# Three weight buffers instead of two, six gathered tokens instead of eight, and later transfers in SyncE's queue

## The chip, the cores and the metric

The kernel runs on one core of one Trainium2 chip. The metric is the device time of one execution in microseconds, given as the median of several runs. The engines are TensorE (PE; its weight loads are PEld), VectorE (DVE), ScalarE (ACT), GpSimd (POOL) and SyncE (SP). Sixteen DMA engines move data between HBM and SBUF; two queues feed them here, SyncE's and GpSimd's.

## What is computed

Two transformer blocks in a row over 256 tokens of width 1024, batch 1, float32. The first has attention with 8 heads of 64, a spatial gating unit and a feed-forward layer. The second has two layers over the tokens (x) and a context of 256 tokens (ctx). Each layer is a mixer (latent attention, a Fourier branch, a convolution branch, merged by gates) and then an expert layer:

```python
    def chunk(hc):
        q = (hc @ w_query).reshape(PEER_CHUNK, PEER_HEADS, 2, D_KEY // 2)
        s = jnp.einsum('chpd,hpnd->chpn', q, sub_keys).astype(jnp.float32)
        s_top, i_top = lax.top_k(s, PEER_TOPK)
...
        best, pos = lax.top_k(cand, PEER_TOPK)
        eid = jnp.take_along_axis(cand_id, pos, axis=-1)
        gate = jax.nn.softmax(best, axis=-1).astype(hc.dtype)
        u = jnp.take(u_tab, eid, axis=0)
        act = jax.nn.gelu(jnp.einsum('chkd,cd->chk', u, hc)) * gate
        v = jnp.take(v_tab, eid, axis=0)
        return jnp.einsum('chk,chkd->cd', act, v)
```

Each token picks 8 x 16 = 128 rows of `u_tab` and 128 rows of `v_tab`, 4 KB each: 0.524 MB per table and token. 768 token steps (ctx layer 0, x layer 0, x layer 1) make 805 MB of gathered rows. Shifts, scales and gates of every norm come from a modulation: a vector times a 1024 x 6144 matrix (`adaln`, and the same in the first block).

## The kernel before, in words

**Weights.** `chunks` is the list of all weight tiles in the order in which TensorE uses them: large ones of 2 MB (1024 x 512) and small ones of 0.5 to 1 MB. SyncE loads tile i into `W[:, i % RING]`, RING = 2, and waits for `w_used` of tile i - RING, which TensorE signals behind a drain (L368) in `done_with_weights`. A merge goes through pairs: a large gate tile ("zg") against H, then a small branch tile ("wb"). There are four merges: "c0" (context, layer 0), "f" (first block), "x0", and "x1", whose stretch has no gathers. In SyncE's queue other transfers stand between the weight tiles: `xT`, the mask, `wsgT` and eight pieces of `b_sgu` (they wait for `idx_ready` 2, the end of the second route), and the sub-keys (they wait for `att_ready`).

**Modulation.** `MODS` lists 18 modulations of 4 MB each, in two halves ("chunks") of 2 MB. All run in the first mixer "c0" and its route, at the places of `MODS_AT`: 0 and 1 at "n1", 2 at "zf", 3 at "dc", 4 at "v", 5 at "heads", 6 at "roots", 7 at "normed", 8 to 12 in the merge, 13 to 17 in the steps "top 0" to "keys 0" of the first route. The halves lie in UV, the buffer of the gathered rows, which is not used before: 4 x 16 KB per partition. GpSimd loads them (L1940) and waits for `rows_copied`, which ScalarE signals when it has copied a modulation's rows to `yfill`. TensorE's `modulation` (matmuls at L508) waits for both halves, then turns the rows of the modulation before it (L492); VectorE's `add_rows` (L1030) adds them.

**Gathered rows.** Visit g handles tokens 2g and 2g + 1. GpSimd gathers U rows (L1961) into slot tok % SLOTS, at most three visits ahead, when `dots` says that token tok - SLOTS is done, and V rows (L1971) when `outputs` says that visit g - SLOTS/2 is done. TensorE spreads the token's h over the partitions (L404), VectorE takes the dot products (L968), ScalarE the gelu, VectorE multiplies by the gate, TensorE sums the V rows (L419) two visits later. Visits are laid into TensorE's program by an estimate, `beat`: one visit per PACE = 7.4 estimated us of products, and at the end of each segment the rest in one stretch (`stream`, `close_stream`). 256 visits belong to segment 0, 128 to segment 1. All of SBUF that matters here is W (RING x 16 KB per partition) and UV (2 x SLOTS x 4 KB).

Of the kernel before, what the change touches and what calls it, by code (L numbers as in the profile page):

```python
# [25 lines left out]
NEXP = NKEY * NKEY  # L26


SLOTS = 8
GROUP = 32  # L30
PAIRS = P // 2
FILL = 64
# [32 lines left out]
def two_blocks_kernel(nc, A, out):  # L65
# [7 lines left out]
    with ctx:  # L73
# [5 lines left out]
        def sem(name):  # L79

            if name not in sems:
                sems[name] = ctx.enter_context(nc.semaphore(name))
            return sems[name]
# [1 line left out]

        X = sb("X", [P, DT, TALL])
        H = sb("H", [P, DT, SEQ])
        RING = 2
        W = sb("W", [P, RING, 4096])
        KC = sb("KC", [QK, MH, SEQ])  # L90
        VC = sb("VC", [P, 2, 512])
        UV = sb("UV", [P, 2 * SLOTS, D])
        hs = sb("hs", [96, 2, 4, D], bf16)
        acts = sb("acts", [P, SLOTS, 2 * GROUP - 1])
        yfill = sb("yfill", [P, 512])
        dots = sb("dots", [P, SLOTS])
        gel = sb("gel", [P, SLOTS])
        idxT = sb("idxT", [P, 2, P], u32)
# [47 lines left out]

        Us, Vs = UV[:, 0:SLOTS, :], UV[:, SLOTS:, :]

        def mod_chunk(i):
            return UV[:, 4 * (i % 4):4 * (i % 4) + 4, :].rearrange("p a b -> p (a b)").rearrange("p (k n) -> p k n", n=512)  # L150


        q1 = view(0, 4, SEQ)
# [87 lines left out]
        MODS = [("l", 0, m) for m in range(6)] + [("ada", 0, m) for m in range(6)] + [("l", 1, m) for m in range(6)]  # L241
# [12 lines left out]
        def cols(ap, j):  # L254
            return ap[:, :, j * 512:(j + 1) * 512]
# [45 lines left out]
        def ring_slot(i):  # L301
            _, _, kt, n = chunks[i]
            return W[:, i % RING, 0:kt * n].rearrange("p (k n) -> p k n", n=n)

# [20 lines left out]
        def _(pe):  # L325
# [3 lines left out]
            pool = list(range(NBANK))  # L329
# [78 lines left out]
            def outputs(g):  # L408
# [5 lines left out]
                for tok in (2 * g, 2 * g + 1):  # L414
                    pe.wait_ge(sem(f"v_arrived{tok % SLOTS}"), 16 * (tok // SLOTS + 1))
                for tok in (2 * g, 2 * g + 1):
# [78 lines left out]
            def modulation(u, flush=False):  # L495

                o = bank(("mr", u))
                if u == 0:
                    pe.wait_ge(sem("cond_ready"), 1)
                w = [mod_chunk(2 * u + j) for j in range(2)]  # L500
                for j in range(2):
                    i = 2 * u + j
                    pe.wait_ge(sem(f"mod_arrived{i % 4}"), 16 * (i // 4 + 1))
                for kk in range(4):
                    for j in range(2):
                        for kh in range(2):
                            q = 32 * (2 * j + kh)
                            last = mm(o[q:q + 32, :], cond32[:, 4 * kh + kk, :], w[j][:, 4 * kh + kk, :], start=(kk == 0), stop=(kk == 3))  # L508
                full(last, ("mr", u))
                if pending:  # L510
                    turn_rows()
                pending.append(u)
                if flush:
                    turn_rows()
# [378 lines left out]
        @block.sync  # L893
        def _(sp):
            sp.dma_start(vec[:, :], A["vec"]).then_inc(sem("vec_loaded"), 16)
            sp.dma_start(ident[:, :], A["ident"]).then_inc(sem("ident_set"), 16)
            sp.dma_start(X[:, :, 0:SEQ], A["ctxT"]).then_inc(sem("ctx_loaded"), 16)

            def weight(i):
                if i >= RING:  # L900

                    sp.wait_ge(sem("w_used"), i - RING + 1)
                sp.dma_start(ring_slot(i), chunks[i][1]).then_inc(sem(f"w_arrived{i % RING}"), 16)

            sp.wait_ge(sem("mod_arrived3"), 16)
            for i in range(RING):
                weight(i)
            sp.dma_start(dftc[:, :, :], A["dftc"]).then_inc(sem("const_loaded"), 16)
            sp.dma_start(ropet[:, :, :], A["rope"][:, :, SEQ:]).then_inc(sem("const_loaded"), 16)
            sp.dma_start(rotm[:, :], A["rotm"]).then_inc(sem("const_loaded"), 16)  # L910
            sp.dma_start(gqk[:, :], A["gqk"]).then_inc(sem("const_loaded"), 16)
            sp.dma_start(iota16[:, :], A["iota16"]).then_inc(sem("const_loaded"), 16)
            attended = {"c0": 8, "x0": 24, "x1": 32}
            for i in range(RING, len(chunks)):
                weight(i)
                what = chunks[i][0]
                if what == ("inC", "c0") or what == ("inB", "c0"):
                    sp.dma_start(X[:, :, SEQ:], A["xT"]).then_inc(sem("x_loaded"), 16)
                if what == ("in1", 1):

                    sp.wait_ge(sem("idx_ready"), 2)
                    sp.dma_start(mask1, A["mask"]).then_inc(sem("mask_loaded"), 16)
                    sp.dma_start(wsg1, A["wsgT"]).then_inc(sem("wsg_loaded"), 16)
                    for p in range(4):
                        for a in range(2):
                            sp.dma_start(bsg1[64 * a:64 * a + 64, p, :], A["b_sgu"][0, 2 * p + a:2 * p + a + 1, :].to_broadcast([64, P])).then_inc(sem("bsg_loaded"), 16)
                if what[0] == "wb" and what[1] in attended and what[2:] == (0, 0):

                    sp.wait_ge(sem("att_ready"), attended[what[1]])
                    sp.dma_start(keys, A["keys"][LAYER[what[1]]]).then_inc(sem("keys_loaded"), 16)  # L930
            sp.wait_ge(sem("added"), 12)
            sp.dma_start(out, X[:, :, SEQ:]).then_inc(sem("stored"), 16)
            sp.wait_ge(sem("stored"), 16)
# [995 lines left out]
        @block.gpsimd  # L1929
        def _(pool):  # L1930
            def load_mods(u):

                which, l, m = MODS[u]
                src = rows(A["w_ada"][0] if which == "ada" else A["w_mod_2"][l])
                for j in range(2):
                    if u >= 2:

                        pool.wait_ge(sem("rows_copied"), u - 1)
                    i = 2 * u + j
                    pool.dma_start(mod_chunk(i), cols(src, 2 * m + j)).then_inc(sem(f"mod_arrived{i % 4}"), 16)  # L1940

            for u in range(2):
                load_mods(u)
            pool.wait_ge(sem("ones_set"), 1)
            pool.affine_select(out=tri[:, :], in_=ones[:, :], compare_op=ALU.is_ge, fill=0.0, base=0,
                               pattern=[[1, P]], channel_multiplier=-1).then_inc(sem("tri_set"), 1)
            for u in range(2, len(MODS)):
                load_mods(u)
            pool.wait_ge(sem("rows_copied"), len(MODS))

            def gather_u(g):

                if 2 * g % P == 0:
                    pool.wait_ge(sem("idx_ready"), 2 * g // P + 1)
                for tok in (2 * g, 2 * g + 1):
                    j = tok % SLOTS
                    if tok >= SLOTS:
                        pool.wait_ge(sem("dots"), tok - SLOTS + 1)
                    pool.sem_inc(sem("pool_paced"), 1)
                    off = bass.IndirectOffsetOnAxis(idxT[:, tok // P % 2, tok % P:tok % P + 1], 0)  # L1960
                    pool.indirect_dma_start(Us[:, j, :], None, A["u_tab"], off).then_inc(sem(f"u_arrived{j}"), 16)  # L1961

            def gather_v(g):

                if g >= SLOTS // 2:
                    pool.wait_ge(sem("outputs"), g - SLOTS // 2 + 1)
                pool.sem_inc(sem("pool_paced"), 1)
                for tok in (2 * g, 2 * g + 1):
                    j = tok % SLOTS
                    off = bass.IndirectOffsetOnAxis(idxT[:, tok // P % 2, tok % P:tok % P + 1], 0)  # L1970
                    pool.indirect_dma_start(Vs[:, j, :], None, A["v_tab"], off).then_inc(sem(f"v_arrived{j}"), 16)  # L1971

            asked = 0
            for g0, g1 in SEGMENTS:
                for g in range(g0, g1):
                    for ahead in range(asked, min(g + 3, g1)):
                        n = ahead // PAIRS
                        if ahead > g and ahead % PAIRS < 2 and ready_at[n] > PAIRS * n - 2:
                            break
                        gather_u(ahead)  # L1980
                        asked = ahead + 1
                    gather_v(g)
# [72 lines left out]
```

## Time and profile before

| | |
|---|---|
| median of 3 runs | 3815.41 us (3814.5 to 3819.07) |
| profiled execution | 3841.13 us, its span 3839.4 us |
| PE busy | 2670.4 us (70%) |
| PEld busy | 1375.4 us (36%) |
| DVE busy | 1781.0 us (46%) |
| POOL busy | 1478.2 us (39%) |
| ACT busy | 497.7 us (13%) |
| DMA | 1047.09 MB, mean 273 GB/s |
| granted TensorE clock, mean | 0.786 |

The profiled execution is one run with the hardware profiler on, and somewhat longer than the median. The first 480 us are "c0" and its first route, then the first block and the mixer "x0" with visits among the products, from about 1830 to 2620 mostly visits, from 2620 to 3070 the mixer "x1" without visits, and to the end visits alone. The mean GB/s hides these stretches.

### The profile page before, as it was taken

How to read it: one execution, taken by the hardware profiler on the slowest of the kernel's cores; microseconds unless marked ns; L12 is line 12 of the kernel's file. 1: busy time of each engine (PE TensorE's matmuls, PEld its weight loads, DVE VectorE, ACT ScalarE, POOL GpSimd, SP SyncE). 2: the span in 40 equal slices, each digit the busy share in tenths (PEclk: the TensorE clock that was granted, in tenths of full speed). 3: DMA queues.
4: the chain of work that ended last, by engine and by line, in shares of the span. 5: the costliest groups of instructions: out<-in, count | busy, mean ns of one | idle time of the engine just before them, and what ended most of it. 6: DMA issues, size and time to landing. Idle time of an engine off the chain costs nothing.

```text
span 3839.4 us, 35128 instructions
## 1 busy us (share of the span) xinstructions
PE 2670.4 (70%) x11672; PEld 1375.4 (36%) x11672; DVE 1781.0 (46%) x4443; ACT 497.7 (13%) x1114; POOL 1478.2 (39%) x1577
## 2 busy tenths in 40 slices
PE   7798676889998888784565555557788455555555
PEld 4376443466776436562121000004377400000000
DVE  2602673624234673256765444443711784444444
ACT  2301020401001231010020000002210100000000
POOL 1000052434334333241546666661000156666665
PEclk9899887899999979896576666668699756666666
DMA  8765477779899757682889999993023189999998
GB/s 305 264 247 208 176 281 254 249 281 342 327 342 337 271 188 258 241 301 84 305 314 337 357 355 358 356 357 132 33 93 137 41 320 355 349 359 361 349 361 323
DMA packets 325907, 1047.09 MB, mean 273 GB/s; under 512 B 27424, under 2 KB 38752, under 8 KB 325728
## 3 DMA queue, kind: packets, MB, share of 16 engines
q0 software_dynamic: 240192, 880.90, 62.1%
q1 hardware_dynamic: 85536, 163.95, 12.3%
q8 instruction: 94, 1.54, 0.2%
q14 instruction: 85, 0.70, 0.1%
HBM read 1043.70 MB, written 1.05 MB: 272 GB/s over the span
## 4 chain that ended last, share of the span: by engine, by line
PE 34%; DVE 19%; issue 16%; another core or an unknown queue 10%; DMA 8%; PEld 7%; ACT 2%; PEldq 2%; POOL 1%; DVEq 0%; SPq 0%; ACTq 0%; POOLq 0%
PE ps L381 15%; PEld ps L381 7%; PE ps L404 7%; DVE UV L968 6%; PE ps L419 6%; DMA W<-in_w_in 4%; PE ps L373 2%; DMA UV<-in_w_mod 2%; PEldq L368 2%; DVE arena L1210 2%; ACT arena L1545 1%; DMA W<-in_w_out 1%; PE ps L687 1%; DVE arena L1308 1%
## 5 line engine op out<-in xcount | busy, mean ns | idle before, releaser
L968 DVE SCALAR_TENSOR_TENSOR UV<-ps,UV 128x1024 f32<-128x1024 f32 x768 | 913.7, 1222 | 1163.0 <-PE ps L404 559.5
L1961 POOL DMA_INDIRECT UV<-in_u_tab,idxT x768 | 723.8, 942 | 1527.7 <-DVE UV L968 730.4
L404 PE MATMUL ps<-hs,selb 96*128 96x512 bf16 x1536 | 581.3, 491 | 684.9 <-issue 361.8
L1971 POOL DMA_INDIRECT UV<-in_v_tab,idxT x768 | 721.9, 940 | 408.9 <-issue 209.3
L381 PE MATMUL ps<-H,W 128*128 128x256 f32 (+2 forms) x3296 | 693.8, 373 | 87.8 <-DMA W<-in_w_in 61.9
L381 PEld LDWEIGHTS ps<-H,W 128*128 128x128 f32 (+1 forms) x3296 | 593.5, 201 | 206.3 <-DMA W<-in_w_in 67.6
L404 PEld LDWEIGHTS ps<-hs,selb 96*128 96x128 bf16 x1536 | 124.2, 107 | 1256.0 <-issue 626.6
L419 PE MATMUL ps<-UV,acts 128*32 128x512 f32 x3072 | 542.5, 787 | 40.8 <-issue 31.2
L381 PE MATMUL ps<-arena,W 128*128 128x256 f32 (+1 forms) x1632 | 376.3, 388 | 27.7 <-DMA W<-in_w_out 18.0
L381 PEld LDWEIGHTS ps<-arena,W 128*128 128x128 f32 (+1 forms) x1632 | 307.8, 192 | 117.9 <-issue 75.8
L1545 ACT ACTIVATE arena<-ps 128x512 f32<-128x512 f32 (+7 forms) x310 | 167.5, 550 | 1078.0 <-PE ps L381 838.8
L1545 ACT ACTIVATE gel<-dots 128x2 f32<-128x2 f32 x384 | 77.5, 202 | 1539.8 <-DVE UV L968 814.7
L419 PEld LDWEIGHTS ps<-UV,acts 128*32 128x32 f32 x3072 | 68.5, 122 | 275.4 <-issue 272.3
L1110 DVE SCALAR_TENSOR_TENSOR arena<-arena,ps 128x512 f32<-128x512 f32 x44 | 30.3, 688 | 268.7 <-PE ps L381 267.2
L1940 POOL DMA_DIRECT2D UV<-in_w_mod x24 | 21.4, 897 | 272.1 <-ACTq L1597 271.3
L508 PE MATMUL ps<-UV,cond 128*32 128x512 f32 x576 | 76.7, 676 | 27.5 <-DMA UV<-in_w_mod 25.6
L1545 ACT ACT_TABLE_LOAD x69 | 88.5, 1283 | 16.0 <-PE ps L548 11.3
L1210 DVE SCALAR_TENSOR_TENSOR arena<-arena,vec 128x256 f32<-128x256 f32 x180 | 79.3, 482 | 3.2
L780 PE MATMUL ps<-ident,arena 128*128 128x128 f32 x6 | 2.7, 450 | 106.6 <-DVEq L1388 104.0
L687 PE MATMUL ps<-arena,ident 8*96 8x512 f32 x56 | 48.1, 989 | 28.7 <-DVEq L1263 21.5
L373 PE MATMUL ps<-W,H 128*128 128x256 f32 (+1 forms) x160 | 52.9, 489 | 20.5 <-DMA W<-in_w_in 19.4
L1129 DVE SCALAR_TENSOR_TENSOR X<-ps,half,X 128x256 f32<-128x256 f32 x32 | 14.0, 479 | 111.3 <-PE ps L381 111.3
(165 smaller groups left out, 1735.9 us busy)
## 6 DMA issues: line engine op xcount, KB each, us to landing
W<-in_w_in SPq DMA_DIRECT2D x30, 2048.0 KB
UV<-in_w_mod POOLq DMA_DIRECT2D x24, 2048.0 KB, 14.1
W<-in_w_ff SPq DMA_DIRECT2D x16, 2048.0 KB
UV<-in_w_ada POOLq DMA_DIRECT2D x12, 2048.0 KB, 12.1
W<-in_w_out SPq DMA_DIRECT2D x8, 2048.0 KB
W<-in_w_query SPq DMA_DIRECT2D x6, 2048.0 KB
UV<-in_u_tab,idxT POOLq DMA_INDIRECT x768
UV<-in_v_tab,idxT POOLq DMA_INDIRECT x768
```

What stands on the lines that cost most here:

```text
L368: pe.drain().then_inc(sem("w_used"), 1)
L373: last = mm(o, lhs[k], rhs[k], start=(k == 0), stop=(k == n - 1))
L381: last = mm(o, w[:, k, col:col + m], src[:, k, c], start=(k == 0), stop=(k == kt - 1))
L404: last = mm(ps[:, HB + 2 * (tok % 2) + hf, :], one, hs[:, n % 2, t // GROUP, hf * 512:(hf + 1) * 512], start=True, stop=True)
L419: last = mm(ps[q:q + GROUP, YB, :], acts[:, tok % SLOTS, GROUP - 1 - r:2 * GROUP - 1 - r], Vs[:, tok % SLOTS, hf * 512:(hf + 1) * 512], st ...
L508: last = mm(o[q:q + 32, :], cond32[:, 4 * kh + kk, :], w[j][:, 4 * kh + kk, :], start=(kk == 0), stop=(kk == 3))
L687: full(mm(o[0:QK, :], ident[0:8, i:i + 1].to_broadcast([8, QK]), hrs[:, :], start=True, stop=True), (tag, "hb", i))
L968: dve.scalar_tensor_tensor(out=Us[:, j, :], in0=ps[:, b:b + 2, :].rearrange("p a b -> p (a b)"), scalar=1.0, in1=Us[:, j, :], op0=MUL, op1 ...
L1210: last = dve.scalar_tensor_tensor(out=a, in0=u, scalar=wt, in1=a, op0=MUL, op1=ADD)
L1545: return act.activation(o, i, f, **kw)
L1961: pool.indirect_dma_start(Us[:, j, :], None, A["u_tab"], off).then_inc(sem(f"u_arrived{j}"), 16)
L1971: pool.indirect_dma_start(Vs[:, j, :], None, A["v_tab"], off).then_inc(sem(f"v_arrived{j}"), 16)
```

## The change

RING becomes 3 and SLOTS becomes 6: W grows by 16 KB per partition and UV shrinks by 16 KB. The modulation's halves have SLOTS // 2 = 3 buffers. The waits follow: the three first weight tiles wait for three halves, not four; half i waits until modulation (i - 3) // 2 is copied. The transfers between weight tiles move one or two places down in the list of tiles, so that they still stand behind tiles that are already asked for.

```diff
-SLOTS = 8
+SLOTS = 6
-        RING = 2
+        RING = 3
+        MODBUF = SLOTS // 2
         def mod_chunk(i):
-            return UV[:, 4 * (i % 4):4 * (i % 4) + 4, :].rearrange("p a b -> p (a b)").rearrange("p (k n) -> p k n", n=512)
+            return UV[:, 4 * (i % MODBUF):4 * (i % MODBUF) + 4, :].rearrange("p a b -> p (a b)").rearrange("p (k n) -> p k n", n=512)
...
-                    pe.wait_ge(sem(f"mod_arrived{i % 4}"), 16 * (i // 4 + 1))
+                    pe.wait_ge(sem(f"mod_arrived{i % MODBUF}"), 16 * (i // MODBUF + 1))
...
-            sp.wait_ge(sem("mod_arrived3"), 16)
+            sp.wait_ge(sem(f"mod_arrived{MODBUF - 1}"), 16)
...
-                if what == ("inC", "c0") or what == ("inB", "c0"):
+                if what == ("dft", "c0"):
                     sp.dma_start(X[:, :, SEQ:], A["xT"]).then_inc(sem("x_loaded"), 16)
-                if what == ("in1", 1):
+                if what == ("in1", 3):
...
-                if what[0] == "wb" and what[1] in attended and what[2:] == (0, 0):
+                if what[0] == "zg" and what[1] in attended and what[2:] == (0, 1):
...
-                    if u >= 2:
-
-                        pool.wait_ge(sem("rows_copied"), u - 1)
                     i = 2 * u + j
-                    pool.dma_start(mod_chunk(i), cols(src, 2 * m + j)).then_inc(sem(f"mod_arrived{i % 4}"), 16)
-            for u in range(2):
-                load_mods(u)
+                    if i >= MODBUF:
+
+                        pool.wait_ge(sem("rows_copied"), (i - MODBUF) // 2 + 1)
+                    pool.dma_start(mod_chunk(i), cols(src, 2 * m + j)).then_inc(sem(f"mod_arrived{i % MODBUF}"), 16)
+            load_mods(0)
             pool.wait_ge(sem("ones_set"), 1)
...
-            for u in range(2, len(MODS)):
+            for u in range(1, len(MODS)):
                 load_mods(u)
```

SyncE's queue around the first block, before: `in_w_in` tiles are in1 0 to in1 4, the first row of each piece holds the two query tiles of "c0".

```order
L903 DMA W<-in_w_query_2 128x8x512 [waits w_used] x2
L903 DMA W<-in_w_in 128x8x512 [waits w_used] x2
L922 DMA arena<-in_mask 128x512 [waits idx_ready]
L923 DMA arena<-in_wsgT 128x1024
L926 DMA arena<-in_b_sgu 64x128 x8
L903 DMA W<-in_w_in 128x8x512 [waits w_used] x4
```

The same place of SyncE's queue in the changed kernel:

```order
L905 DMA W<-in_w_query_2 128x8x512 [waits w_used] x2
L905 DMA W<-in_w_in 128x8x512 [waits w_used] x4
L924 DMA arena<-in_mask 128x512 [waits idx_ready]
L925 DMA arena<-in_wsgT 128x1024
L928 DMA arena<-in_b_sgu 64x128 x8
L905 DMA W<-in_w_in 128x8x512 [waits w_used] x2
```

The ten small transfers with their wait for `idx_ready` stood behind two of the first block's tiles; now they stand behind four.

TensorE at the first two modulations of "c0", before (16 matmuls for each; L492 turns the rows):

```order
L508 MATMUL ps<-UV,cond32 32x512 [waits mod_arrived1,mod_arrived0,cond_ready]
L508 MATMUL ps<-UV,cond32 32x512 x15
L508 MATMUL ps<-UV,cond32 32x512 [waits mod_arrived3,mod_arrived2]
L508 MATMUL ps<-UV,cond32 32x512 x15
L492 MATMUL ps<-ident,yfill 128x128 [waits rows_copied]
```

And in the changed kernel:

```order
L510 MATMUL ps<-UV,cond32 32x512 [waits mod_arrived1,mod_arrived0,cond_ready]
L510 MATMUL ps<-UV,cond32 32x512 x15
L510 MATMUL ps<-UV,cond32 32x512 [waits mod_arrived0,mod_arrived2]
L510 MATMUL ps<-UV,cond32 32x512 x15
L494 MATMUL ps<-ident,yfill 128x128 [waits rows_copied]
```

The second modulation's second half now lies in buffer 0, which the first modulation has just read.

## Rows read from the trace of the kernel before

**Rows 1.** Page, part 2: GB/s of the DMA in 40 equal slices.

```profile
GB/s 305 264 247 208 176 281 254 249 281 342 327 342 337 271 188 258 241 301 84 305 314 337 357 355 358 356 357 132 33 93 137 41 320 355 349 359 361 349 361 323
```

**Rows 2.** Busy us of each engine in three stretches, then PE clock, DMA share, GB/s.

```profile
896.00:1215.00 319.00, 308.44 (x1503) 224.40 (x1501) 107.21 (x224) 35.73 (x85) 126.86 (x136) 0.99 0.91 335
1475.00:1700.00 225.00, 185.36 (x837) 133.00 (x835) 65.14 (x126) 15.42 (x37) 68.74 (x74) 0.90 0.73 262
3120.00:3830.00 710.00, 376.55 (x1466) 58.85 (x1470) 331.48 (x718) 29.05 (x127) 446.05 (x476) 0.66 0.95 354
```

**Rows 3.** Waits of the whole span: us in total, times, longest.

```profile
PE ps L381 <- DMA W<-in_w_in: 61.9, 15, 8.4
...
PE ps L381 <- DMA W<-in_w_out: 18.0, 4, 5.6
```

**Rows 4.** Chain (start, us, what), then TensorE's timeline, in "x0" and "x1".

```profile
1547.01 12.21 DMA W<-in_w_in
...
2859.56 8.05 DMA W<-in_w_in
...
2867.65 15.77 PE L381 MATMUL ps<-H,W 128*128 128x256 f32 x64 [4.22 <-DMA W<-in_w_in]
...
2891.87 14.08 PE L381 MATMUL ps<-H,W 128*128 128x256 f32 x64 [1.05 <-DMA W<-in_w_in]
```

**Rows 5.** Timeline of SyncE and of TensorE at the first block's third tile.

```profile
599.73 0.34 SPq L922 DMA_DIRECT2D arena<-in_mask  x1
...
616.69 10.10 PE L373 MATMUL ps<-W,H 128*128 128x512 f32 x16 [19.41 <-DMA W<-in_w_in]
```

**Rows 6.** The start: chain, then GpSimd, TensorE and ScalarE in order of time.

```profile
29.46 11.43 DMA W<-in_w_in
...
30.95 1.80 POOL L1940 DMA_DIRECT2D UV<-in_w_mod  x2 [25.43 <-ACTq L1597]
...
26.23 7.07 PE L508 MATMUL ps<-UV,cond 128*32 128x512 f32 x64
...
40.93 30.67 PE L381 MATMUL ps<-H,W 128*128 128x256 f32 x128 [5.52 <-DMA W<-in_w_in]
...
36.63 4.04 ACT L1545 ACTIVATE H<-H,mod,gs 128x256 f32<-128x256 f32 x8 [2.04 <-DVEq L1062]
```

**Rows 7.** Timeline of GpSimd and of TensorE at modulations 3, 4 and 7.

```profile
83.98 1.75 POOL L1940 DMA_DIRECT2D UV<-in_w_mod  x2 [47.23 <-ACTq L1597]
...
158.11 1.76 POOL L1940 DMA_DIRECT2D UV<-in_w_ada  x2 [24.62 <-ACTq L1597]
...
90.57 3.64 PE L508 MATMUL ps<-UV,cond 128*32 128x512 f32 x32
...
100.59 5.24 PE L508 MATMUL ps<-UV,cond 128*32 128x512 f32 x32 [4.07 <-DMA UV<-in_w_mod]
...
160.52 3.64 PE L508 MATMUL ps<-UV,cond 128*32 128x512 f32 x32
```

**Rows 8.** Timeline of GpSimd and TensorE at modulations 15 to 17.

```profile
419.39 1.76 POOL L1940 DMA_DIRECT2D UV<-in_w_mod  x2 [102.54 <-ACTq L1597]
...
441.39 1.75 POOL L1940 DMA_DIRECT2D UV<-in_w_mod  x2 [16.09 <-ACTq L1597]
...
433.83 5.87 PE L508 MATMUL ps<-UV,cond 128*32 128x512 f32 x32 [11.39 <-DMA UV<-in_w_mod]
...
444.66 5.34 PE L508 MATMUL ps<-UV,cond 128*32 128x512 f32 x32 [4.37 <-DMA UV<-in_w_mod]
...
456.33 6.56 PE L508 MATMUL ps<-UV,cond 128*32 128x512 f32 x32 [5.75 <-DMA UV<-in_w_mod]
```

**Rows 9.** Timeline of GpSimd and VectorE in the last stretch.

```profile
3295.25 0.94 POOL L1961 DMA_INDIRECT UV<-in_u_tab,idxT  x1 [1.79 <-DVE UV L968]
...
3315.96 0.94 POOL L1971 DMA_INDIRECT UV<-in_v_tab,idxT  x1 [3.61 <-remote]
...
3315.30 1.23 DVE L968 SCALAR_TENSOR_TENSOR UV<-ps,UV 128x1024 f32<-128x1024 f32 x1 [7.21 <-remote]
```

## The prediction

> **What bounds the kernel now.** I read the bandwidth line of the page first, then the table of stretches, the waits of TensorE, and the order of time at the places that the diff touches. The bandwidth line [rows 1] shows three kinds of stretch: some at 340 to 361 GB/s, some near 250, and a hole in slices 28 to 32. The table [rows 2] makes it sharp. In the feed-forward stretch (896 to 1215) TensorE is busy nearly all the time and the DMA moves 335 GB/s beside it: nothing is to be won there. In the last stretch (3120 to 3830) only gathers run: 354 GB/s, DMA share 0.95. The stretch from 2060 to 2620 reads alike in slices 22 to 27 of [rows 1]. The merge of "x0" (1475 to 1700) is neither: 262 GB/s, and TensorE's clock below 1.
>
> Why it is neither is in the waits of TensorE [rows 3]: 15 waits for `in_w_in` tiles at L381 (61.9 us), four for `in_w_out` (18.0); one more stands at L373 (19.4) [rows 5]. One of the 15, 5.5 us in front of the first product (40.93), belongs to another matter [rows 6]. The remaining 93.8 us sit in the merges and at the first block's third weight tile. Each is one pattern [rows 4]: a large tile may be asked for only when the tile two places back is released, and between them stands a short product (L381 on `arena`, 3.7 us). The load takes 8.05 us from its issue, the cover is shorter, and TensorE stands for 4.2 us. After it, the same 64 matmuls take 15.77 us, where after a wait of 1.05 they take 14.08. So a longer wait costs 1.5 to 3 us more than its idle time. I read that extra behind all 16 waits longer than 2 us: 34 us in sum.
>
> **Part 1, the third weight buffer.** Tile i is asked for when tile i-3 is released, so a large tile has the previous large product as cover too: 14 + 3.7 = 17.7 us in "x1" against the 8.05 of the load. With gathers beside it the cover is longer (the visits between the products) and the chain puts such a load at 12.21 us; both fit. Removed: 93.8 + 34 = 128 us. In "x0" this needs bandwidth: 262 GB/s x 225 us = 59 MB, now in 225 - 50 = 175 us, which is 337 GB/s. The feed-forward row shows 335 without such waits, and 354 is shown elsewhere, so I take nearly all: 120. Bounds: two thirds (80, the gathers take their share) and 128.
>
> The 19.4 us at 616 are of this kind for another reason [rows 5]: SyncE stands at the mask's transfer until `idx_ready` (599.73), and the third and fourth tile are queued behind it. The change moves that wait behind in1 3, and with three buffers tiles 2 and 3 are asked for while the first route still runs. What the wait now holds back is tile 4: issued after the ten small transfers (near 606), needed after two products of about 18 us each (14 and two visits) that start at 616.69 - 19.41 = 597.3. Hidden. Mask and `bsg1` still leave at 600, needed after all three products. The sub-keys move behind one more large tile, for a wait on attention that ended long before their use; `xT` moves by one small tile, and its reader is the norm of the first block, far behind. Nothing for these.
>
> **Part 2, the modulation in three buffers of 2 MB instead of four.** A modulation reads two buffers. So far the next pair was there ahead; now half of modulation u+1 may be asked for only when the rows of modulation u are copied. Where two modulations stand near each other, TensorE waits for a 2 MB load. Its length: a pair issued at 419.39 is complete at 433.83 and the next at 444.66, 10.8 us later, so 5.4 per buffer. If the queue works in order, the first of a lone pair lands 5.4 before 433.8: 9.0 us after its issue [rows 8]. If both advance together it is 14.4. I take 9.0. The Trainium skill, "DMA: Bandwidth & Descriptors", Anatomy of one DMA (SWDGE path), fits a DMA as 2.0 us and its bytes over 436e3 us: an estimate of 6.8 us for 2 MB, which would make the six such waits below some 13 us cheaper in all; the trace's 9.0 stands.
>
> - First norm [rows 6]. The second half of modulation 1 can be issued when the rows of modulation 0 are copied, at 30.95, beside three weight tiles that leave near 24 (29.46 less one buffer of 5.4, since they wait for three, not four). Beside such traffic the first weight tile took 11.43. So it lands near 41 (39 to 42), its matmuls take 5, and H follows some 4 us on (the 64 matmuls from 26.23 are over at 33.3, H follows from 36.63): first product at about 50 against 40.93. +9 (7 to 11).
> - Place "v" [rows 7]. Modulation 3's second half leaves at 84, lands at 93, needed at 90.57: +2 and a slow start. Modulation 4's leaves at 99.5, lands at 108.5 against 100.59. VectorE adds the rows of modulation 3 only behind modulation 4's matmuls, and the convolution branch stands behind that. +8 (6 to 10).
> - Place "normed" [rows 7]. Modulation 7 starts at 160.52; its half leaves when modulation 6 is copied, at 158.11, and lands at 167, slow start. Attention is queued behind it. +6. Modulations 8 to 12 have a merge product of 14 us and a short one between them: hidden.
> - The first route [rows 8]. Modulation 14 ran without a wait, over before 422. Its half now leaves at 419.4 and lands at 428.4. From there each modulation takes 5.9 (matmuls) + 1.7 (439.7 to 441.39, copy and issue) + 9.0 = 16.6 us where it took 10.8. The last starts at 428.4 + 3 x 16.6 = 478.2 instead of 456.33. VectorE adds its rows in program order, the last three steps of the route stand behind, and the first gather behind them. +21 (18 if a few us hide elsewhere; 30 if both halves advance together).
>
> Sum of part 2: 9 + 8 + 6 + 21 = 44 (7 + 6 + 4 + 18 = 35 to 11 + 10 + 8 + 30 = 59).
>
> **Part 3, six tokens of gathered rows instead of eight.** In the middle stretches visits are 9 us apart and three of them cover a gather. In the last stretch it is open. GpSimd issues a gather every 1.24 us (0.94 busy, 0.30 between), 14 in a row from 3295.25 on, then stands 3.61 us at a V gather (3315.96), which the order shows to wait for `outputs`; VectorE stands 7.21 us at the same time [rows 9]. The mean is 0.524 MB / 354 GB/s = 1.48 per gather, so the stalls are 0.24 x 16 = 3.8 us per 16 gathers, as many as there are slots (8 U, 8 V). If the stall comes once per filling of the slots, 12 slots give 1.24 + 3.8 / 12 = 1.56: +0.08. 476 gathers stand in this stretch [rows 2], and 560 us at the same rate make another 378: 854 x 0.08 = +68. Lower bound 0: the rate is the DMA's, whose share is 0.95. I take a good third, +25, since the DMA's share leaves at most 5% idle.
>
> **Sum.** -120 + 44 + 25 = -51 us, against the profiled execution's 3841.1 (span 3839.4): 3790. The runs' median is 3815.4, 0.7% below the profiled one, so I predict 3815 - 51 = 3764 us.
>
> **The rivals.**
> (a) The gathers pay full price, +68: -8 us, 3807. For: GpSimd's regular stall at `outputs`. Against: the DMA's share.
> (b) The weights only move their wait: the third load runs at the same time as the gathers and both slow down, half of the 120 comes back: +9, 3824. For: 337 GB/s is needed where 262 runs. Against: the feed-forward row. The Trainium skill, "DMA: Bandwidth & Descriptors", Specifications, puts the HBM limit of a core near 358 GB/s; by that rule the merges still fit, narrowly, and the trace agrees (354 in the last stretch).
> (c) Slower: the stall of the gathers does not get rarer or shorter but longer, because four issues that covered it (5.0 us) are gone. (3.8 + 5.0) / 12 + 1.24 = 1.97 per gather would be +418 us at worst. Without part 3 the sum is -120 + 44 = -76, so it decides from 0.10 us per gather on (76 + 8 of the bound below, over 854); at 0.2 it is +171 - 76 = +95, 3910. For: VectorE, TensorE and GpSimd stand together for several us, and only what is already issued feeds the DMA then. Against: TensorE and VectorE are busy 53% and 47% there and need three visits ahead, which six tokens hold.
>
> **How the numbers follow.** A difference within 0.2% (8 us) can't be told from none. My forecast, 3722 to 3790: 0.54. (a), 3795 to 3815, either faster or same: 0.16. (b), around no change: 0.10. (c): 0.20. So faster 0.65, same 0.13, slower 0.22. Low end: -128 + 35 + 0 = -93, 3722. High end: -80 + 50 + 68 = +38, 3853; it also takes in the beginning of (c).
>
> **What the profile of the changed kernel would show.** Part 1: no wait on W at L381 and L373 above 2 us except the first; a merge stretch of "x1" 27 us shorter; the third tile of the first block starts near 597 relative to the transposes of `eid`. Part 2: waits on `UV<-in_w_mod` or `in_w_ada` at the matmuls of modulations 1, 3, 4, 7 and 14 to 17, with the first gather some 38 us later than before (44, less 6 for the first `w_out` wait). Part 3: between 0 and 0.08 us more per gather in the last stretch, 345 to 354 GB/s. The prediction is wrong if that last stretch falls below 330 GB/s, or if the weight waits reappear as waits for U or V in the merges.

## The result, and the profile after

The changed kernel takes 3752.94 us, median of 4 runs (3746.12 to 3757.7), the kernel before 3815.85 on the same chip. The ratio is 0.9833, with a 95% interval of 0.9814 to 0.9851, so 63 us less. A later timing (after2, below) gave 0.9813 (0.9795 to 0.983). The prediction was 3764 (51 less), faster.

Page of the changed kernel, part 2, then its busy time in three stretches that answer to those of [rows 2] (columns as there):

```profile
GB/s 257 264 200 281 170 189 298 272 322 350 327 348 314 297 207 253 332 319 137 287 320 334 355 359 363 359 361 130 53 96 123 71 317 363 355 362 366 356 366 321
```

```profile
890.00:1210.00 320.00, 310.02 (x1506) 225.21 (x1504) 107.78 (x226) 35.44 (x84) 127.44 (x136) 0.99 0.91 332
1467.00:1644.00 177.00, 171.19 (x823) 124.33 (x822) 61.27 (x118) 12.23 (x33) 67.46 (x72) 0.99 0.90 325
3040.00:3750.00 710.00, 397.80 (x1474) 66.51 (x1474) 329.69 (x713) 29.53 (x128) 447.74 (x478) 0.65 0.95 355
```

The first and the third row read as before. The middle one is the merge of "x0": the same work in 177 us instead of 225, at 325 GB/s instead of 262, and with a granted clock of 0.99 instead of 0.90.

Waits of the changed kernel's TensorE in that merge (us in total, times, longest). Before, five waits for `in_w_in` (31.0 us) and one for `in_w_out` (5.6) stood in this stretch. Now nothing here is above 4 us, and there is no row for W:

```profile
PE ps L383 <- issue: 3.5, 12, 0.4
PE ps L383 <- DVEq L1118: 2.3, 1, 2.3
PE ps L536 <- DVEq L1140: 0.3, 1, 0.3
```

The same in the merge of "x1", TensorE in order of time; [rows 4] has a large product with its wait (4.22 and 15.77 us):

```profile
2841.66 3.69 PE L383 MATMUL ps<-arena,W 128*128 128x256 f32 x16 [0.26 <-issue]
2845.61 14.05 PE L383 MATMUL ps<-H,W 128*128 128x256 f32 x64 [0.26 <-issue]
```

The wait is gone and the product takes 14.05: 4 us of idle time and 1.7 of slow start, both back.

What part 2 costs stands in the waits of the whole span. The first row was 25.6 us in 4 waits before. The second was 8.8 us in 5 waits at eight slots:

```profile
PE ps L510 <- DMA UV<-in_w_mod: 64.0, 7, 13.5
PE ps L421 <- DMA UV<-in_v_tab,idxT: 242.6, 112, 5.5
```

TensorE at modulations 1, 4 and 7, and at 15 to 17 of the first route:

```profile
43.33 6.44 PE L510 MATMUL ps<-UV,cond 128*32 128x512 f32 x32 [13.47 <-DMA UV<-in_w_mod]
...
120.45 5.43 PE L510 MATMUL ps<-UV,cond 128*32 128x512 f32 x32 [9.20 <-DMA UV<-in_w_mod]
...
187.41 6.08 PE L510 MATMUL ps<-UV,cond 128*32 128x512 f32 x32 [6.68 <-DMA UV<-in_w_ada]
...
467.27 6.10 PE L510 MATMUL ps<-UV,cond 128*32 128x512 f32 x32 [9.85 <-DMA UV<-in_w_mod]
...
483.63 6.45 PE L510 MATMUL ps<-UV,cond 128*32 128x512 f32 x32 [9.68 <-DMA UV<-in_w_mod]
...
500.37 4.91 PE L510 MATMUL ps<-UV,cond 128*32 128x512 f32 x32 [9.71 <-DMA UV<-in_w_mod]
```

TensorE executes the same 11,672 matmuls in the same order in both kernels. So the start of one and the same matmul can be compared, and the difference read where each part acts. The table is worked out from the two traces:

| place (us in the trace before) | later (+) or earlier (-) there, in all | change in this stretch |
|---|---|---|
| first products of "c0" (50) | +10.8 | +10.8 |
| behind the place "v" (141) | +20.0 | +9.2 |
| behind "normed" (202) | +26.9 | +6.9 |
| merge of "c0" (352) | +22.6 | -4.3 |
| end of the first route (479) | +42.4 | +19.8 |
| just ahead of the first block's third tile (577) | +37.1 | -5.3 |
| first block's third tile (617) | +17.5 | -19.6 |
| first block's merge (890) | -5.1 | -22.6 |
| start of the merge of "x0" (1475) | -4.2 | +0.9 |
| behind it (1747) | -54.3 | -50.1 |
| first product of "x1", behind the first gathers-only stretch (2635) | -52.1 | +2.2 |
| behind the merge of "x1" (2944) | -75.8 | -23.7 |
| last matmul | -83.5 | -7.7 |

The sum, 83.5, is more than the 63 of the medians, because the profiled execution of before was itself 26 us above its median (3841.1 against 3815.4) and that of the changed kernel only 5 (3757.7 against 3752.9). A trace of six slots alone (gat6, below), a kernel timed as equal, is 24.1 us shorter than the trace of before: by the same matmuls it is 5 to 6 us ahead from the stretch between 495 and 510, 5 more by the merge of "x0", another 5 in that merge and 7 in the last stretch. The rows at 577 and at the last matmul are of that kind, and so are some 5 of the 50.1 us of "x0". Against the traces of gat6, of its repetition and of mod3 (below), "x0" gives 44 to 46, and the five stretches with weight waits ("c0", the third tile, the first block's merge, "x0", "x1") give 112 to 118 in sum, where the table has 120.

### The profile page after: what moved, and what is told of

It reads as the page before. It is cut to its first block, busy times and chain, and to the rows that moved or that the text cites. A ratio compares the mean times of both kernels' runs of the same rounds, so it can differ in the third digit from the quotient of the medians.

```text
span 3756.0 us, 35129 instructions
## 1 busy us (share of the span) xinstructions
PE 2674.5 (71%) x11672; PEld 1360.6 (36%) x11672; DVE 1780.1 (47%) x4443; ACT 497.8 (13%) x1114; POOL 1478.0 (39%) x1577
## 4 chain that ended last, share of the span: by engine, by line
PE 47%; DVE 19%; issue 12%; another core or an unknown queue 11%; DMA 4%; POOL 4%; ACT 2%; ACTq 0%; DVEq 0%; POOLq 0%; SPq 0%
PE ps L383 26%; DVE UV L970 6%; PE ps L421 5%; PE ps L406 5%; PE ps L375 3%; PE ps L510 2%; POOL UV L1972 2%; DMA UV<-in_v_tab,idxT 2%; DMA UV<-in_w_mod 2%; POOL UV L1962 2%; DVE arena L1212 1%; ACT arena L1547 1%; PE ps L689 1%; DVE arena L1313 1%
## 5 line engine op out<-in xcount | busy, mean ns | idle before, releaser
L421 PE MATMUL ps<-UV,acts 128*32 128x512 f32 x3072 | 568.5, 821 | 285.2 <-DMA UV<-in_v_tab,idxT 242.6
L383 PE MATMUL ps<-H,W 128*128 128x256 f32 (+2 forms) x3296 | 667.4, 363 | 32.3 <-ACT H L1547 19.5
L383 PEld LDWEIGHTS ps<-H,W 128*128 128x128 f32 (+1 forms) x3296 | 573.7, 195 | 143.2 <-issue 73.7
L510 PE MATMUL ps<-UV,cond 128*32 128x512 f32 x576 | 85.7, 743 | 72.5 <-DMA UV<-in_w_mod 64.0
L1942 POOL DMA_DIRECT2D UV<-in_w_ada x12 | 10.6, 890 | 155.6 <-ACTq L1599 155.6
L510 PEld LDWEIGHTS ps<-UV,cond 128*32 128x32 f32 x576 | 23.1, 132 | 126.8 <-issue 126.7
```

Of the source, the lines that this page charges most:

```text
L383: last = mm(o, w[:, k, col:col + m], src[:, k, c], start=(k == 0), stop=(k == kt - 1))
L421: last = mm(ps[q:q + GROUP, YB, :], acts[:, tok % SLOTS, GROUP - 1 - r:2 * GROUP - 1 - r], Vs[:, tok % SLOTS, hf * 512:(hf + 1) * 512], st ...
```

## The experiments

**Six tokens alone (gat6).** The kernel before; the buffer keeps its size.

```diff
-SLOTS = 8
+SLOTS = 6
...
-        UV = sb("UV", [P, 2 * SLOTS, D])
+        UV = sb("UV", [P, 16, D])
...
-        Us, Vs = UV[:, 0:SLOTS, :], UV[:, SLOTS:, :]
+        Us, Vs = UV[:, 0:SLOTS, :], UV[:, SLOTS:2 * SLOTS, :]
```

> The kernel before, with six tokens of gathered rows instead of eight and nothing else: the buffer keeps its size, so the modulation has its four buffers, and the weights have two. Theory 1 (the stretches with gathers alone are bound by the DMA or by something that counts gathers, not slots): 3816 us, within 8, and in the stretch of gathers alone GpSimd's long waits still come once in 16 gathers. Theory 2 (my prediction's term): +25, 3841. Rival (a) of the prediction (one stall for each filling of the slots, so once in 12 gathers): +68, 3884.

Measured: 3820.82, ratio 1.0005 (0.9992 to 1.0018). Repeated on another chip:

> Six tokens of gathered rows alone, once more. Theory 1: no difference to the kernel before on either chip, within 0.2%. Rival (part 3's cost shows only where the gathers are quicker, as four tokens cost 2.2% there): 0.3 to 1% slower on a chip with 1.29 us per gather.

Measured: 3826.93, ratio 1.0015 (1.0002 to 1.0027), so 0 to 10 us. The second chip had slow gathers too; the case of quick gathers was not met. Of GpSimd in 100 us of the last stretch of gat6, the gathers that stood over 2 us:

```profile
3220.29 0.94 POOL L1971 DMA_INDIRECT UV<-in_v_tab,idxT  x1 [3.79 <-remote]
...
3243.61 0.93 POOL L1971 DMA_INDIRECT UV<-in_v_tab,idxT  x1 [3.76 <-remote]
...
3266.97 0.94 POOL L1971 DMA_INDIRECT UV<-in_v_tab,idxT  x1 [3.80 <-remote]
...
3290.81 0.94 POOL L1971 DMA_INDIRECT UV<-in_v_tab,idxT  x1 [3.48 <-remote]
```

They are 23.3 to 23.8 us apart, with 16 gathers between them, as with eight slots. The stall does not come once per filling of the slots: 12 slots do not make it more frequent.

**Three modulation buffers alone (mod3).** The kernel before, with the halves in three buffers and the waits as in the changed kernel (three of its edits):

```diff
-            return UV[:, 4 * (i % 4):4 * (i % 4) + 4, :].rearrange("p a b -> p (a b)").rearrange("p (k n) -> p k n", n=512)
+            return UV[:, 4 * (i % 3):4 * (i % 3) + 4, :].rearrange("p a b -> p (a b)").rearrange("p (k n) -> p k n", n=512)
...
-                    pe.wait_ge(sem(f"mod_arrived{i % 4}"), 16 * (i // 4 + 1))
+                    pe.wait_ge(sem(f"mod_arrived{i % 3}"), 16 * (i // 3 + 1))
...
-                    if u >= 2:
-                        pool.wait_ge(sem("rows_copied"), u - 1)
                     i = 2 * u + j
+                    if i >= 3:
+                        pool.wait_ge(sem("rows_copied"), (i - 3) // 2 + 1)
```

> The kernel before, with the modulation's halves in three buffers and nothing else (eight tokens, two weight buffers). Theory 1 (the ledger of the two traces: +10.8 at the first norm, +9.2 at the place v, +6.9 at the place normed, +14 to +20 in the first route, each on the path to the first gather): the first gather 40 to 46 us later, the time 3816 + 43 = 3859, 3852 to 3862. Rival (it is made good behind the route, where the weights or the transfer of the mask were waited for anyway): under +15, below 3831.

Measured: 3859.74, ratio 1.0099 (1.0081 to 1.0117): +38 (31 to 45). The waits of its TensorE:

```profile
PE ps L508 <- DMA UV<-in_w_mod: 62.5, 7, 13.5
PE ps L381 <- DMA W<-in_w_in: 56.1, 13, 8.6
```

The new waits are those of the changed kernel, and the old ones for W are still there.

**The place of the mask (oldmask).** The changed kernel with one line back:

```diff
-                if what == ("in1", 3):
+                if what == ("in1", 1):
```

> The changed kernel, but SyncE's wait for idx_ready with the mask's and the other nine transfers back behind the first block's second tile. Theory 1 (the 19.5 us at the first block's third tile come from the place of this wait, not from the number of buffers): the wait of TensorE for that tile is back, 15 to 20 us, 3753 + 17 = 3770. Rival (a third buffer alone would cover it): within 5 of 3753.

Measured: 3767.04, ratio to before 0.9863 (0.9843 to 0.9883), 0.3% or 11 us above the ratio of the changed kernel in the first timing, and 19 above the one in the second. TensorE at the first block's third tile:

```profile
653.10 9.74 PE L375 MATMUL ps<-W,H 128*128 128x512 f32 x16 [19.05 <-DMA W<-in_w_in]
```

The wait of [rows 5] (19.41) is back, whatever the number of buffers. In this trace 19 us appear there and 12 are left at the end. The wait puts the rival out; the ratio alone would not do it against the first timing of the changed kernel, since the two intervals overlap.

**A third buffer without the earlier request (lateask).** The changed kernel, each tile asked for one tile later:

```diff
-                    sp.wait_ge(sem("w_used"), i - RING + 1)
+                    sp.wait_ge(sem("w_used"), i - RING + 2)
```

> The changed kernel with its three weight buffers, but each tile is asked for one tile later (when the tile two places back is released, as before), so the third buffer gives no time. Theory 1 (all of part 1 in the merges is the earlier request): the waits of TensorE for W at L383 are back, some 14 to 16 of them and 65 to 80 us, and about 100 us of time (x0 50, x1 24, first block's merge 21, c0 4): 3753 + 100 = 3853, 3840 to 3860. Rival (part of the gain comes from the smaller gather buffer or from other spacing): under 3830.

> Each weight tile asked for one tile later, once more, for a chip on which the changed kernel was timed too (the first run of it was on a chip where gathers alone are quicker). Theory 1 (part 1 is the earlier request; the late mask stays): ratio to the kernel before 1.005 to 1.01, that is 2.3 to 2.8% above the changed kernel's 0.982, some 3845. Rival (on such a chip part of the gain is the smaller gather buffer's): ratio under 1.0.

Measured: 3677.83 and 3672.39, ratios 1.0099 (1.0082 to 1.0117) and 1.0088 (1.0074 to 1.0103). Both times the chip was one on which the kernel before takes 3640 us, so the difference to the changed kernel has to go by ratios: 1.009 against 0.982, 2.7%. This assumes that the changed kernel's ratio is the same there, which was not timed. Its waits, from the second run:

```profile
PE ps L383 <- DMA W<-in_w_in: 62.3, 14, 8.5
...
PE ps L383 <- DMA W<-in_w_out: 16.9, 4, 5.9
```

The waits of [rows 3] are back, but for the one at L373. Matmul by matmul against the trace "base" of the same chip (the kernel before, below), lateask gains nothing in the merges: in "x0" it goes from +33.0 to +33.3, where the changed kernel went from -4.2 to -54.3; in "x1" from +36.9 to +36.4. Only the third tile of the first block is quicker (+49.8 to +30.3, the mask). lateask2 says the same (+23.1 to +21.7, +24.6 to +26.5, +44.2 to +24.6). So a third buffer that is filled late gives nothing in the merges; the time of the request gives it.

**The modulation's fourth buffer, lent by W (borrow).** W's third buffer takes every fourth half until modulation 17 is copied, and serves the weights from the first block's third tile on. The transfers of `xT` and of the sub-keys of "c0" stand earlier in SyncE's queue again, since "c0" has two buffers:

```diff
-        MODBUF = SLOTS // 2
+        MODBUF = 4
...
+            if i % MODBUF == 3:
+                return W[:, 2, :].rearrange("p (k n) -> p k n", n=512)
...
+        FIRST3 = chunk_at["in1", 2]
+        slot_of = [i % 2 if i < FIRST3 else (i - FIRST3 + 2) % 3 for i in range(len(chunks))]
...
+                if i == FIRST3:
+                    sp.wait_ge(sem("rows_copied"), len(MODS))
+                elif before_of[i] >= 0:
+                    sp.wait_ge(sem("w_used"), before_of[i] + 1)
```

> The changed kernel, but the third weight buffer holds every fourth half of the modulation until the last modulation is read; weights use two buffers up to the first block's second tile and three from its third tile on. Theory 1 (the loss of part 2 is only for want of the fourth buffer): the first gather at about 485 instead of 523, the weight waits in the merge of c0 back (+4), the rest as in the changed kernel: 3753 - 43 + 4 = 3714, 3708 to 3722. Rival (the loss is made good later whatever happens, since the visits or the DMA catch up): 3745 to 3757.

> The changed kernel with the third weight buffer lent to the modulation, once more. Theory 1: 30 to 40 us below the changed kernel on either chip (35 on the first), since the first 530 us hold no gathers; on a chip with 3640 for the kernel before that is 3540. Rival: the gain is made good by then.

Measured: 3718.25, ratio 0.9724 (0.9702 to 0.9746), and 3709.28, 0.971 (0.969 to 0.973). That is 35 us below the changed kernel's first median and 40 below its second, which was taken on the same chip, and the fastest version here. By the same matmuls all of it is there at the end of the first route: the two kernels are 36.6 us apart at that place and 35.6 at the end. Its waits for W in the merge of "c0" came back, as expected:

```profile
PE ps L391 <- DMA W<-in_w_in: 8.4, 2, 8.3
PE ps L391 <- DMA W<-in_w_out: 4.1, 1, 4.1
```

**The changed kernel once more (after2).**

> The changed kernel once more. On the chip of the runs lateask, gat4 and base the kernel before takes 3640 us instead of 3820, and its trace shows the whole difference in the stretches of gathers alone (1.29 us per gather instead of 1.47). Theory 1 (no part of the change works in those stretches; parts 1 and 2 act where both chips run alike): on such a chip 3640 - 65 = 3575, and 100 us below lateask; on a chip like the first, ratio 0.983 again. Rival (with quicker gathers six tokens cover less, and the gain shrinks): 3600 or more.

It ran on a chip with slow gathers: 3748.88, ratio 0.9813 (0.9795 to 0.983). The changed kernel was not timed on the quick chip. A bound for six slots there can be read from lateask and lateask2 against "base", by the same matmuls: in the first gathers-only stretch they lose 3.6 and 2.9 us, behind the mixer "x1" 1.3 and 2.3, so some 5 us in each trace.

**Four tokens (gat4).** As gat6, with `SLOTS = 4`.

> The kernel before, with four tokens of gathered rows (buffer size, modulation and weights as before). Theory 1 (the DMA or something that counts gathers sets the rate, and slots matter only when they cover less than the round trip): within 1% of 3820 if GpSimd's long waits still come every 16 gathers; the more so, the more six slots had to spare. Rival (slots are near their limit): four slots make GpSimd wait for dots or outputs at nearly each visit, and the last stretch goes from 1.47 to over 1.6 us per gather, over 3930.

Measured on the chip with quick gathers: 3724.88, ratio 1.0225 (1.0207 to 1.0243), +82. By the same matmuls, 14 us are lost by 930, some 6 more by 1470, 38 from there to the end of the first gathers-only stretch and 26 behind the mixer "x1". Between 3150 and 3550 it moves 397 GB/s against 409 with eight slots, so a visit (four gathers) takes 5.28 us instead of 5.13. So the slots are near their limit at four and not at six: lateask2, with six, has 409 GB/s too (3200 to 3600). Both theories missed: the loss is more than the 1% of the first, and the last stretch, at 1.32 us per gather, is far from the 1.6 of the second.

**The kernel before on that chip (base).**

> The kernel before once more, for a second trace. The first one's execution was 0.7% above the median; theory 1 (the trace of before had slow stretches by chance): here a span 10 to 25 us shorter, with the difference in the stretches of gathers alone. Rival (profiling always costs it that): the same 3839 again.

It took 3642.17 (a single run) and its span was 3640.4, 199 us shorter than the trace of before: neither theory. Its stretch of gathers alone:

```profile
3150.00:3550.00 400.00, 256.10 (x940) 49.91 (x936) 194.09 (x407) 16.81 (x80) 292.85 (x313) 0.66 1.03 409
```

**Half the rows (half).** `idxT[0:64, ...]` into `Us[0:64, ...]` and `Vs[0:64, ...]`, with all that reads them cut to 64 partitions: the kernel leaves out half of each token's rows.

> The changed kernel, each gather of 64 rows instead of 128 (half of every token's experts are left out: 0.262 MB per gather; dot products, gelu, gate and sums over 64 partitions only). Theory 1 (GpSimd's long wait once in 16 gathers comes from the bytes or rows in flight, as the DMA is the bound): with half the bytes the waits vanish or come every 32, and the stretch of gathers alone runs at GpSimd's 1.24 to 1.30 us per gather. Rival (the wait counts gathers or visits, whatever they carry): still every 16, with 1.4 or more per gather.

It took 3568.0 (a single run). It ran on the chip without regular stalls, so it says nothing on the stall of every 16. What it shows instead stands at the end.

## Why the prediction was right, point by point

**Part 1, taken as -120: right.** The table gives -4.3 in "c0", -19.6 at the third tile, -22.6 in the first block's merge, -50.1 in "x0" and -23.7 in "x1": -120.3. The prediction had 50 for "x0" and 27 for "x1". Part of the agreement is that forecast and table start from the same slow trace of before: against the other traces "x0" gives 44 to 46. The extra for the slow start, 34 us beside 93.8 of idle time, exists ("x0" gains 44 to 50 where 36.6 us of waits went, and a product of "x1" takes 14.05 instead of 15.77) but was put too high: five stretches that give 112 to 120 had 93.8 us of waits, which leaves 18 to 26. Against mod3, which has the same modulation waits, the profiled changed kernel is 112 us shorter, and the ratios of the medians differ by 2.7 to 2.9% (101 to 109 us; the six slots are in this difference, at next to nothing). So -120 is at the upper end of what was measured, and what was measured is above the 80 of the rival case. The bandwidth step held: 337 GB/s in 175 us were worked out for "x0", 325 GB/s in 177 us were measured. The cause in the merges, a request one tile earlier, is shown by lateask and lateask2. The mask's share is shown by oldmask.

**Part 2, taken as +44: right.** By place, predicted and read: first norm +9, +10.8; "v" +8, +9.2; "normed" +6, +6.9; first route +21, +19.8. Sum +46.7 in the profile, +38 in the medians of mod3. In the route I had modulations 16.6 us apart. They start at 451.25, 467.27, 483.63 and 500.37, 16.0 to 16.7 apart. What I took for the load, 9.0, was the choice between 9.0 and 14.4: TensorE stands 9.7 to 9.9 there. The Trainium skill's fit ("DMA: Bandwidth & Descriptors", Anatomy of one DMA) gives an estimate of 6.8 for such a load; the chain of the changed kernel has one at 12.25, beside the first weight loads, and seven others at 8.4 to 9.7, of which this is one:

```profile
94.79 8.71 DMA UV<-in_w_mod
```

The measurement decides, and it is longer.

**Part 3, taken as +25: wrong in mechanism and size.** The step that failed is "if the stall comes once per filling of the slots, 12 slots give 1.24 + 3.8 / 12". The stall comes once in 16 gathers at six slots as at eight. That 16 was also the number of slots was a coincidence, and I had divided the stall by it. gat6 measured +2 and +6 us (the intervals reach from -3 to +10). My lower bound, 0, was about the right value, and an argument for it, the DMA's share of 0.95, stood in the text; that the DMA is what sets the rate there is not shown, since the cause of the stall was not found.

**Sum.** -120 + 44 + 25 = -51 was predicted; measured were -63 and -71. mod3 splits what was measured: +38 for part 2, and from there to the changed kernel -101 to -109 for parts 1 and 3 together, of which gat6 gives +2 to +6 to part 3. So part 1 is about -109 by the medians. (The split adds up by the way it is made and is no test of the sum.) Part 3 was 19 to 23 us too high and part 2 some 6, while part 1 was some 11 too favourable: that the total came within 11 to 20 us is in part luck, as errors of both signs met. The upper end of the range, +38, took +50 for part 2 where its own bound was +59; with that it would have been +47, which changes nothing here.

**The rivals.** (a), 3807, and (c), the longer stall, fell with gat6: no price per gather at six slots. Too few slots do cost time, but farther down: four cost 2.2% on the quick chip. (b), half of part 1 lost to contention, fell with the row of "x0". Of the Trainium skill's limit near 358 GB/s for a core ("DMA: Bandwidth & Descriptors", Specifications) I had said that the trace agrees. The base row shows 409 GB/s on another chip, so it is no limit there, and on the chip of the changed kernel's trace slices reach 366.

**The signs.** No wait for W was left: right. The waits of the modulations stand where they were expected (1, 3, 4, 7 and 14 to 17). The first gather was expected some 38 us later: it came 42.4 later. The merge of "x1" was to be 27 us shorter: 23.7. The last stretch was to stay between 345 and 354 GB/s: it has 355. A sign that I had not named is the 242.6 us of TensorE's waits for V rows. gat6 has it too (252.7 us, where the kernel before has 8.8) and loses next to nothing, so it replaces other waits of the same cycle; which ones was not followed.

## What to carry to other kernels

With a buffer of two tiles and products of unequal length, look at what stands between the release of a buffer and the next large tile; if it is shorter than the load, a third buffer pays the wait and the slow start of the engine behind it. Where the memory for it comes from must be priced by who else used it, and in what phase: here a second user needed the space only at the start, so lending the new buffer to it until then gave another 35 to 40 us. A stall's period that equals some number of buffers is no proof that these buffers cause it; changing the number by itself tells.

## What the runs showed of the hardware

**Chips differ.** The kernel before took 3815 to 3822 us on three occasions and 3640 to 3642 on two others, both on one chip. In the feed-forward stretch both run at 333 to 334 GB/s; the difference lies in the stretches of gathers alone, 357 GB/s and 1.46 to 1.48 us per gather against 409 GB/s and 1.29. The regular stall of GpSimd every 16 gathers (23.3 to 23.8 us) is there on the former only. What makes it was not found: six or eight slots make no difference to it. Where the stall is missing, GpSimd issues one gather after the other, 1.24 us each (0.93 or 0.94 busy and 0.30 between), of the 1.29 that a gather takes, so there its own pace may be the limit and not the DMA:

```profile
3204.30 0.93 POOL L1961 DMA_INDIRECT UV<-in_u_tab,idxT  x1 [0.30 <-issue]
```

**Half the partitions, half the rate.** The run "half" in the stretch that is shown above for "base", 64 rows per gather, then one of its gathers:

```profile
3150.00:3550.00 400.00, 293.80 (x943) 53.21 (x943) 193.74 (x406) 16.83 (x80) 275.10 (x308) 0.50 1.02 204
```

```profile
3203.57 0.90 POOL L1962 DMA_INDIRECT UV<-in_u_tab,idxT  x1 [0.30 <-issue]
```

The DMA engines read as busy (1.02) as with 128 rows (1.03 in "base") and move 204 GB/s instead of 409; a gather takes 1.28 to 1.29 us in both. That the time did not fall has two possible reasons, which this run does not part: the transfers themselves, for which the busy share speaks, and the pace of GpSimd, which issues a gather every 1.20 us here (0.90 and 0.30) and waits for hardly anything else. The second is what the expectation had as its theory 1, and the time came out as it says. The Trainium skill, "SBUF — State Buffer", Door 1, has a DMA's rate depend on how many of SBUF's ports its partitions reach; the trace agrees with that in size (204 of 409 GB/s at an equal busy share), though no run here tries another set of 64 partitions or a slower pace of issue.
